# One step of a hybrid decoder on one core: in the last stage GpSimd adds the x2 rows, and VectorE closes each tile two tiles behind its gating

## The reference

```
x = x + gt_m * y                                  # x2, the rows behind the mixer
h = rmsnorm(x, g_ffn) * (1 + sc_f) + sh_f
x = x + gt_f * moe(h, ...)                        # x3 = x2 + gt_f * (routed + shared)
y_prompt = rmsnorm(xp, g_final)                   # x3 * rsqrt(mean(x3 * x3) + EPS) * g_final
y_sample = rmsnorm(xs, g_final)
```

## Time and profile before

| what | us |
|---|---|
| timed runs, median of 3 (lowest, highest) | 1517.27 (1516.01, 1518.21) |
| profiled execution, its own time | 1520.14 |
| its span, first to last instruction | 1518.3 |
| busy over the span: PE, DVE, POOL, ACT | 1364.2, 802.8, 440.7, 217.8 |

### The profile page before, as it was taken

One profiled execution on the slowest core, in us unless ns is written; L12 is line 12 of the kernel. 1 busy time (PEld: TensorE's weight loads), 2 busy tenths in 40 slices (PEclk: granted clock), 3 DMA queues, 4 the chain that ended last, 5 costly groups with the idle time before them and its releaser, 6 DMA issues.

```text
span 1518.3 us, 17393 instructions
## 1 busy us (share of the span) xinstructions
PE 1364.2 (90%) x5860; PEld 619.5 (41%) x5860; DVE 802.8 (53%) x2070; ACT 217.8 (14%) x365; POOL 440.7 (29%) x379
## 2 busy tenths in 40 slices
PE   4898999999989999898989997998979999789946
PEld 2344454545545554454633342332323333233313
DVE  1047686988988899887113333242323333333328
ACT  1111213223131313132010000000000000000003
POOL 0000110111111111224134453544444544443410
PEclk8999999999999999999999998999999999999978
DMA  9987311120120101811978998999999999999977
GB/s 331 330 309 265 137 56 58 43 72 31 70 73 28 33 28 53 267 45 57 350 291 320 369 367 323 374 383 345 377 358 359 380 361 364 344 378 355 369 210 283
DMA packets 95386, 362.32 MB, mean 239 GB/s; under 512 B 18157, under 2 KB 32465, under 8 KB 70607
## 3 DMA queue, kind: packets, MB, share of 16 engines
q1 hardware_dynamic: 73191, 306.17, 52.3%
q0 software_dynamic: 20944, 50.89, 13.1%
q10 hardware_dynamic: 1168, 4.23, 0.7%
HBM read 317.61 MB, written 60.10 MB: 249 GB/s over the span
## 4 chain that ended last, share of the span: by engine, by line
PE 39%; DMA 27%; DVE 18%; issue 8%; SPq 4%; ACT 2%; POOL 1%; POOLq 0%; DVEq 0%; ACTq 0%
DMA acc_rows<-xr,kT 10%; PE U L1005 10%; DMA acc_rows<-W,kT 9%; PE U L718 9%; DVE cv L1430 7%; PE R L815 7%; PE R L1021 4%; PE X L754 3%; DMA front<-h_rows,q_r 2%; SPq L432 2%; DMA W<-in_w_ada 2%; DMA W<-in_w 2%; PE R L682 1%; PE U L764 1%; SPq L438 1%
## 5 line engine op out<-in xcount | busy, mean ns | idle before, releaser
L718 PE MATMUL U<-W,front 128*128 128x512 f32 x768 | 344.9, 603 | 1.2 <-issue 1.2
L1430 DVE SCALAR_TENSOR_TENSOR cv<-win,cw,cv 128x128 f32<-128x128 f32 x960 | 256.7, 350 | 1.4
L1005 PE MATMUL U<-W,cat 128*32 128x512 f32 (+2 forms) x1056 | 203.4, 614 | 23.6 <-issue 23.6
L1005 PE MATMUL U<-W,front 128*32 128x512 f32 (+2 forms) x848 | 208.3, 613 | 13.9 <-issue 13.2
L718 PEld LDWEIGHTS U<-W,front 128*128 128x128 f32 x768 | 145.5, 194 | 169.0 <-issue 169.0
L1021 PE MATMUL R<-W,glu 128*32 128x512 f32 (+2 forms) x952 | 208.2, 597 | 1.3 <-DVE glu L1740 1.3
L1727 DVE STREAM_TRANSPOSE front<-front 128x1024 f32<-128x1024 f32 x29 | 59.1, 2037 | 177.3 <-DMA front<-h_rows,q_r 177.3
L1727 DVE STREAM_TRANSPOSE cat<-W 128x1024 f32<-128x1024 f32 x28 | 57.4, 2049 | 148.2 <-DMA W<-h_rows,q_r 148.2
L1986 POOL DMA_INDIRECT front<-h_rows,q_r x116 | 117.1, 1010 | 63.9 <-issue 34.8
L1005 PEld LDWEIGHTS U<-W,front 128*32 128x32 f32 (+2 forms) x848 | 76.6, 145 | 125.2 <-issue 122.4
L1986 POOL DMA_INDIRECT W<-h_rows,q_r x112 | 112.9, 1008 | 44.2 <-issue 33.9
(11 more groups left out here) (371 smaller groups left out, 1215.9 us busy)
## 6 DMA issues: line engine op xcount, KB each, us to landing
W<-in_w SPq DMA_DIRECT2D x192, 1024.0 KB, 17.4
W<-in_w_ada SPq DMA_DIRECT2D x24, 1024.0 KB, 9.4
W<-in_w_in SPq DMA_DIRECT2D x6, 2048.0 KB, 19.9
W<-acc_rows SPq DMA_DIRECT2D x16, 512.0 KB, 9.6
front<-in_x_prompt SPq DMA_DIRECT2D x8, 512.0 KB
W<-in_w_out SPq DMA_DIRECT2D x1, 4096.0 KB, 18.6
xr<-in_x_prompt SPq DMA_DIRECT2D x8, 512.0 KB, 4.1
x_rows<-xr SPq DMA_DIRECT2D x8, 512.0 KB, 3.3
```

Of the source, the lines that this page charges most:

```text
L718: last = mm(U[BANK[g]][:, :], hT[:, k, :], w_in[:, k, 512 * g:512 * g + 512], start=k == 0, stop=k == KT - 1)
L1005: last = mm(U[1][cols, :], xgT[z][:, k, cols], w13[:, :, k, :], start=k == 0, stop=k == KT - 1)
L1430: ins = v.scalar_tensor_tensor(cv[:, c, :], win[:, c, w:w + P], cw[:, c, w:w + 1], cv[:, c, :], ALU.mult, ALU.add)
```

## The change

VectorE's instruction of step 3 is taken out. GpSimd gets it, at the end of its program, with a wait for the x2 rows once and for the gating of each tile. VectorE no longer waits for its own gating, and closes tile i-2 behind the gating of tile i, so two closings are left at the end.

```diff
--- before.py
+++ after.py
@@ -1915,10 +1915,9 @@
                     dve.wait_ge(sum_done, i)
                     ins = v.tensor_tensor(acc_t[i], (X, R)[i % 2][:, :], gt_f, ALU.mult)
                 ins.then_inc(gated, 1)
-                dve.wait_ge(gated, i + 1)
-                v.tensor_tensor(acc_t[i], acc_t[i], x2_t[i], ALU.add).then_inc(x3_ready, 1)
-                if i > 0:
-                    finish(i - 1)
+                if i > 1:
+                    finish(i - 2)
+            finish(TP - 2)
             finish(TP - 1)
             dve.wait_ge(fin_std, NT)
             link(v.reciprocal(rstd_f[TP], std_f[TP]))
@@ -2039,6 +2038,11 @@
                                                 bounds_check=2 * TABLE - 1, oob_is_err=False,
                                                 compute_op=ALU.add).then_inc(scattered[0], 16)
 
+            pool.wait_ge(x2_in, 16 * (TP + 2))
+            for i in range(TP):
+                pool.wait_ge(gated, i + 1)
+                g_.tensor_tensor(acc_t[i], acc_t[i], x2_t[i], ALU.add).then_inc(x3_ready, 1)
+
```

## The result

| kernel | median us | runs | ratio to the kernel before, 95% interval |
|---|---|---|---|
| before | 1516.01 (1513.23 to 1518.21) | 5 | |
| changed | 1522.98 (1521.18 to 1526.22) | 5 | 1.0051 (1.0035 to 1.0067) |

The change makes the kernel slower by 0.51%, 7.7 us of 1516.01 by the ratio (5.3 to 10.2), 6.97 by the medians. The case behind the forecast of 1517.8 did not come. The time is near that of the first rival, foreseen at 1523.8 with a chance of 0.28, and it lies in the range only because that rival had been let into it.

A forecast was written before the change was run, and what follows sets the result against it. VectorE was taken to bound the tail, TensorE 0.36 us a tile behind. Won 1.86 us, lost 1.13, 1.19 and 0.05, so +0.51 on the 1517.27 median: 1517.8, range 1516.0 to 1524.6.

The forecast's parts named there:

- The case behind the forecast of 1517.8: In the tail, VectorE's closing gets in ahead of GpSimd's sum: +0.51 us, chance 0.62.
- the first rival: At the gatings of tiles 2 to 7 GpSimd gets the port first: 4.70 us a tile, +6.5 us, chance 0.28.
- VectorE bounds the tail: In the last eight tiles VectorE sets the pace at 3.79 us a tile, TensorE following at 3.43.
- GpSimd's sum takes 2.35 us: GpSimd's sum with x2 takes 2.35 us per tile, against 1.22 on VectorE.
- Two SBUF inputs exclude GpSimd's sum: The closing multiplication, both inputs in SBUF, and GpSimd's sum exclude each other, alternating at best every 3.36 us.
- the gating is held too: Rival: the gating's one SBUF input also makes it wait for GpSimd's sum, a pace like the slow rival's; chance 0.02.
- VectorE first: VectorE's closing starts before GpSimd's sum at each gating: won 1.86 us, lost 1.13, 1.19 and 0.05, so +0.51.
- The rival without exclusion: In the tail, GpSimd's sum and VectorE's closing run side by side: -0.68 us, 1516.6, chance 0.06.
- two to one for VectorE: Odds that VectorE wins the port at a gating, with GpSimd 0.02 to 0.04 us ahead on paper.
- the equal start that it lost: A trace row at 290.95 where both engines start together and GpSimd's sum is held, taking 1.82 us.
- the closing after GpSimd's end: A closing multiplication that had to wait ends 1.14 us after GpSimd's sum ends.
- The later place wins nothing by itself: Closing two tiles behind only gives GpSimd's longer sum room; VectorE did not wait for a root before.

The follow-up runs named there:

- e2: The changed kernel, but the closing multiplication reads the gain from a copy in PSUM; 1516.65 us, ratio 1.0007 to the kernel before.
- e1: The changed kernel, but GpSimd's sum also waits for the reciprocal ahead of the closing multiplication; 1515.70 us, ratio 1.0001 to the kernel before.
- e4: Half the change on the kernel before: GpSimd does the sum with x2, VectorE still closes one tile behind; 1522.19 us, ratio 1.0047.
- e3: Half the change on the kernel before: VectorE keeps the sum with x2 but closes two tiles behind; 1516.46 us, ratio 1.0002.
- e8: The changed kernel as it is, run again; 1521.14 us, ratio 1.0050 to the kernel before.
- e7: e2 plus four unread TensorE products ahead of its sums, and tile 7's x2 sum on VectorE; 1513.28 us, ratio 0.9993 to the kernel before.

## Where the prediction was right and where it was wrong, point by point

- **VectorE bounds the tail, and TensorE would bound it at 0.36 us a tile less.** Right: with the exclusion gone (e2) the gatings are 3.43 us apart and wait for TensorE.
- **GpSimd's sum takes 2.35 us, picked up 0.08 us after the gating.** Right: 2.34 to 2.35, and 1486.66 - (1485.35 + 1.23) = 0.08.
- **Two SBUF inputs exclude GpSimd's sum, one in PSUM doesn't.** Right, by e2. The rival "the gating is held too" is out by the gatings of e1.
- **VectorE first: +0.51 us.** Its working was right; e1 makes this case and gives +0.43 in the stretch, with gatings 3.43 apart and the closing of tile 6 stretched to 2.70. The rival without exclusion was put at -0.68 and is e2, -0.74.
- **The step that failed: "two to one for VectorE".** This put the forecast on the wrong one of two cases that were both worked out. The rows in the prediction bracket the turning point between 0 and 0.09 us of lead; it put GpSimd's lead at 0.02 to 0.04 us, and read its place in the first third as odds. The lead was 0.02 or 0.03 and GpSimd won at every one of the twelve meetings in two profiles, and at the seven of e4. With the equal start that it lost, the turning point lies between 0 and 0.02 us. The bracket was also wider than it had to be. The trace of the kernel before holds a meeting with a lead of 0.04 us:

```profile
647.72 1.26 POOL L1942 TENSOR_TENSOR o_t<-o_t,gret 128x512 f32<-128x512 f32 x1
647.76 1.37 DVE L1686 TENSOR_TENSOR W<-W 128x128 f32<-128x128 f32 x1
...
650.51 0.29 DVE L1688 TENSOR_TENSOR W<-W 128x128 f32<-128x128 f32 x1
```

GpSimd keeps its 1.26 us and VectorE's small sum takes 1.37 instead of 0.29. By this row a lead of 0.02 to 0.04 lies in the upper half of what is open, and the prediction's own way of reading odds would have favoured GpSimd. The rule of the Trainium skill that the prediction weighed (SBUF — State Buffer, section SBUF: two separate sides), that whichever starts first holds the port for its length, would have given the right answer; I took one equal start as a ground to doubt it where the start was not equal.
- **The price of that rival.** Foreseen 4.70 us a tile and +6.5, measured 4.64 and +6.08. The term that was off is the closing after GpSimd's end, 1.14 foreseen and 1.07 measured; 0.07 times five is most of it. That the time lies in the range, which ended at 1524.6, owes something to luck: the forecast stood on a median of 1517.27 for the kernel before, which came out as 1516.01 in five runs, and the measured ratio on 1517.27 would give 1525.0.
- **"The later place wins nothing by itself."** Right by e4 (34.95 against 34.76 us); that it costs 0.97 us alone (e3) the prediction didn't price.

What stays open is 1.5 us: the timed difference of the changed kernel is 7.7 and 7.6 us by the two ratios, the stretch has 6.08. Counted from the tables' sum of tile 0 instead, the profiles have 36.41 us before, 44.01 and 44.08 in two of the changed kernel, so 7.60 and 7.67 more. The missing 1.5 us thus stands ahead of the gating of tile 1, which begins 7.73 us after tile 0's sum before and 9.25 and 9.33 after. But e3, where GpSimd has no sums, has 9.47 there and e1 8.75, and there is one profile of the kernel before. So no run shows that the change costs this part.

## What to carry to other kernels

Before moving elementwise work from VectorE to GpSimd, list what VectorE runs meanwhile. In these runs its instructions with two tiles in SBUF excluded a GpSimd sum, and the loser waited to the winner's end. If both are released by the same instruction, look at which starts first: here that decided the whole stage, and a lead of 0.02 us was enough. Put the long one behind the short one with a wait (e1), or give VectorE an operand in PSUM (e2). And look at what bounds the stage next: TensorE was so near that even without any exclusion the stretch became only 0.74 us shorter.

Two input tiles may not be the only case. In the trace of the kernel before, a VectorE operation with one input tile and two columns of scalars starts 0.12 us behind a GpSimd sum and takes 1.23 us, while one of the same kind and size (L1653, at 612.18) takes 0.29 beside an idle GpSimd. No run here tests this:

```profile
646.38 1.26 POOL L1941 TENSOR_TENSOR o_t<-o_t,gret 128x512 f32<-128x512 f32 x1 [19.96 <-DVE o_t L1792]
646.50 1.23 DVE L1685 TENSOR_SCALAR W<-W 128x128 f32<-128x128 f32 x1
```

## What the runs showed of the hardware that I had not expected

A delay of 0.13 us in GpSimd's start (0.02 ahead to 0.11 behind) is worth 5.65 us over six tiles, as the good order keeps itself and the bad one too: in e1 the sum of tile 2 ends at 1489.13, 0.18 us after the end of the next gating (1487.73 + 1.22 = 1488.95). The next closing starts at 1489.06, still ahead of the next sum of GpSimd (1489.17).

TensorE's first sum of the stage, after some 20 idle us, took 5.06, 5.48, 6.67 and 6.62 us in four profiles (before, after, e8, e2), against 3.60 later; it begins at a granted clock of 0.50 (1.2 GHz) and later ones run at 1.00 (2.4 GHz). Stretches of e2, in which this sum begins at 1469.30 (the clock is the third number from the end):

```profile
1470.00:1474.00 4.00, 4.00 (x6) 1.65 (x5) 0.00 (x0) 2.73 (x4) 1.13 (x1) 0.50 1.02 417
1474.00:1478.00 4.00, 4.00 (x10) 1.74 (x10) 1.23 (x1) 0.00 (x0) 0.73 (x1) 0.84 1.03 415
1478.00:1482.00 4.00, 4.00 (x11) 1.72 (x10) 2.35 (x3) 1.44 (x3) 2.69 (x2) 1.00 1.03 410
```

In e7, after 6.73 us of other products, the same sum ran at a granted clock of 1.00 and took 3.70.
